# Column norm statistics, a split down projection, a bank-by-bank residual and a reordered router stage in a two-layer MLA and HGRN2 kernel

## The reference, cut to what matters

```python
def rmsnorm(x, g):
    y = x * rsqrt(mean(x * x, -1) + EPS)
    return y * g

for l in range(2):
    mp, ms = ada(c_ctx, w_ada[l], b_ada[l]), ada(c, w_ada[l], b_ada[l])   # silu(c) @ w + b: 6 x 1024 per group
    hp = rmsnorm(xp, norm_mix[l]) * (1 + mp[1]) + mp[0]                   # same for xs with ms
    # l = 0: cq = rmsnorm(h @ w_dq), q = cq @ w_uq, kv = h @ w_dkv, ckv = rmsnorm(kv[:256]), attention, @ w_o
    # l = 1: z, q, i, g from h; chunkwise scan; rmsnorm per head; * silu(g); @ w_o
    xp = xp + mp[2] * yp
    hp = rmsnorm(xp, norm_ffn[l]) * (1 + mp[4]) + mp[3]
    # l = 0: (silu(h @ w1) * (h @ w3)) @ w2;  l = 1: top-2 of 8 experts of softmax(h @ router)
    xp = xp + mp[5] * fp
y_prompt = rmsnorm(xp, final_norm)                                        # same for xs
```

## Time and profile before

| what | value |
|---|---|
| median of three runs | 1766.38 us |
| profiled execution, its own time | 1766.06 us |
| its span | 1764.3 us |
| TensorE, VectorE, ScalarE busy | 94%, 65%, 55% |
| mean granted TensorE clock | 0.971 |
| read from HBM | 489.42 MB |

### The profile page before, as it was taken

One profiled execution on the slowest core, in us unless ns is written; L12 is line 12 of the kernel. 1 busy time (PEld: TensorE's weight loads), 2 busy tenths in 40 slices (PEclk: granted clock), 3 DMA queues, 4 the chain that ended last, 5 costly groups with the idle time before them and its releaser, 6 DMA issues.

```text
span 1764.3 us, 22742 instructions
## 1 busy us (share of the span) xinstructions
PE 1650.6 (94%) x8760; PEld 1323.4 (75%) x8760; DVE 1145.0 (65%) x1098; ACT 963.5 (55%) x976; POOL 36.9 (2%) x35
## 2 busy tenths in 40 slices
PE   5899989999799878889999999999999999999993
PEld 3755779899545667778888888888888888888883
DVE  2126354444311691258898888888888888888886
ACT  1123353333272233257686776777767776777764
POOL 0000000000001010000000000000000000000000
PEclk8999999999899999879999999999999999999997
DMA  9657447775645013069999999999999999999993
GB/s 345 232 176 277 171 151 273 272 260 211 243 143 191 7 44 143 1 209 370 379 375 383 369 375 383 369 379 381 362 391 377 372 383 373 374 384 362 388 367 138
DMA packets 202842, 501.95 MB, mean 285 GB/s; under 512 B 8575, under 2 KB 12062, under 8 KB 188446
## 3 DMA queue, kind: packets, MB, share of 16 engines
q1 hardware_dynamic: 195710, 481.46, 74.3%
q0 software_dynamic: 3664, 13.11, 2.1%
q10 hardware_dynamic: 3408, 6.56, 1.0%
HBM read 489.42 MB, written 11.68 MB: 284 GB/s over the span
## 4 chain that ended last, share of the span: by engine, by line
PE 44%; issue 13%; DVE 6%; ACT 2%; DMA 1%; POOLq 0%; DVEq 0%; ACTq 0%; POOL 0%
PE banks L617 42%; DVE weights_low L1709 2%; DVE ring L1678 2%; PE banks L1046 1%; ACT weights_high L1324 1%; DVE tokens_low L1715 0%; DVE hidden_low L1777 0%; PE banks L1022 0%; DMA pieces<-expert_rows,arena 0%; DVE arena L1773 0%; ACT hT L1120 0%; DMA arena<-token_rows,arena 0%; PE banks L994 0%; DMA arena<-in_state_hgrn 0%; DMA out<-arena 0%
## 5 line engine op out<-in xcount | busy, mean ns | idle before, releaser
L1709 DVE TENSOR_TENSOR weights_low<-pieces,weights_high 128x2048 fp32r<-128x2048 f32 x340 | 763.3, 2288 | 141.4 <-ACT weights_high L1324 141.4
L1324 ACT CAST weights_high<-pieces 128x2048 fp32r<-128x2048 f32 x340 | 632.2, 1912 | 19.9 <-PE banks L617 13.6
L617 PE MATMUL banks<-weights_high,tokens_high 128*128 128x512 f32 x896 | 355.2, 396 | 1.5 <-DVE tokens_low L1715 1.5
L617 PE MATMUL banks<-weights_low,tokens_high 128*128 128x512 f32 x896 | 350.5, 391 | 0.0
L617 PE MATMUL banks<-weights_high,tokens_low 128*128 128x512 f32 x896 | 349.3, 390 | 0.0
L617 PEld LDWEIGHTS banks<-weights_low,tokens_high 128*128 128x128 f32 x896 | 168.6, 188 | 36.2
L617 PEld LDWEIGHTS banks<-weights_high,tokens_high 128*128 128x128 f32 x896 | 169.1, 189 | 34.7 <-issue 1.6
L617 PEld LDWEIGHTS banks<-weights_high,tokens_low 128*128 128x128 f32 x896 | 168.9, 189 | 33.7
L617 PE MATMUL banks<-weights_high,hidden_high 128*128 128x512 f32 x448 | 175.9, 393 | 2.6 <-DVE hidden_low L1777 2.6
L617 PE MATMUL banks<-weights_low,hidden_high 128*128 128x512 f32 x448 | 174.7, 390 | 0.0
L617 PE MATMUL banks<-weights_high,hidden_low 128*128 128x512 f32 x448 | 174.3, 389 | 0.0
(11 more groups left out here) (227 smaller groups left out, 1848.4 us busy)
## 6 DMA issues: line engine op xcount, KB each, us to landing
pieces<-in_moe_w SPq DMA_DIRECT2D x340, 1024.0 KB, 7.5
ring<-in_w_ada SPq DMA_DIRECT2D x24, 2048.0 KB, 9.0
ring<-in_ffn_w SPq DMA_DIRECT2D x15, 2048.0 KB, 8.3
ring<-in_hg_w_f SPq DMA_DIRECT2D x4, 2048.0 KB, 15.2
ring<-in_mla_w_o SPq DMA_DIRECT2D x2, 2048.0 KB, 8.1
ring<-in_hg_w_i SPq DMA_DIRECT2D x2, 2048.0 KB, 14.6
ring<-in_hg_w_q SPq DMA_DIRECT2D x2, 2048.0 KB, 11.1
ring<-in_hg_w_g SPq DMA_DIRECT2D x2, 2048.0 KB, 7.8
```

What stands on the lines that cost most here:

```text
L617: return pe.matmul(o_, lhsT=l, rhs=r, start=start, stop=stop, skip_group_check=True)
L1324: act.copy(parts_hi[:, p % PARTS, :], raw[:, p % RAW, :]).then_inc(rounded, 1)
L1709: dve.tensor_tensor(parts_lo[:, p % PARTS, :], raw[:, p % RAW, :], parts_hi[:, p % PARTS, :].bitcast(F32), ALU.subtract).then_inc(split, 1)
```

## The change

Norm statistics: the squares become the stationary operand and one column of ones the moving one, so the sums of a group stand in one PSUM column with the tokens on the partitions. ScalarE takes the root of 128x2 values straight from PSUM, VectorE the reciprocal, and TensorE spreads it over the partitions again by two products with the identity (`norm_spread`); VectorE reads that from PSUM. ScalarE's table for the root is loaded ahead (`load_root`). Norm 5 stays as it was. Norm 3 writes `x_hi` in the shift itself, and VectorE forms `x_lo` chunk by chunk between the scalings. The start loads `x` first and waits for nothing before the weights; the modulation blocks come in the order 2, 3, 0, then `dq`, then 1, and `dq` is formed in two halves of the features with block 1's step between. The dense residual goes bank by bank, and TensorE no longer waits for all of it. In the router stage the logits come first and are formed chunk by chunk, two pieces rather than four are split ahead, the others after expert 0's tokens, and half of the token rows are turned behind the slot table. The final norm loses a step on VectorE.

```diff
-        add_ada(0, 0, NA_FIRST)
+        ADA_FIRST = (2, 3, 0, 1)
+        add_ada(0, 0, 3)
         add(("dq",), kmaj(a["mla_w_dq"][0], slice(0, QL)))
+        add_ada(0, 3, NA_FIRST)
         add(("dkv",), kmaj(a["mla_w_dkv"][0], slice(0, KVL + ROPE)))
...
+            for g, name in enumerate(("x_prompt", "x_sample")):
+                sp.dma_start(x_rows[:, g, :], a[name][0]).then_inc(rows_in, 16)
             for row, name in ((R_C, "c"), ...
-            for g, name in enumerate(("x_prompt", "x_sample")):
-                sp.dma_start(x_rows[:, g, :], a[name][0]).then_inc(rows_in, 16)
-            sp.wait_ge(consts_in, 16)
-            sp.wait_ge(rows_in, 16 * 11)
...
-                    last = mm(bank[7][:, 0:T], ones[:, :], src[:, k, :], k == 0, k == kc - 1)
+                    for g in range(G):
+                        last = mm(norm_bank[i][:, g:g + 1], src[:, k, P * g:P * g + P], ones[:, 0:1], k == 0 and g == 0, k == kc - 1)
                 last.then_inc(nsum, 1)
+            def norm_spread(i):
+                pe.wait_ge(nrec, NORM_COUNT[i])
+                for g in range(G):
+                    last = mm(norm_bank[i][:, T + P * g:T + P * g + P], inverse[:, g:g + 1].broadcast_to([P, P]), ident, True, True)
+                last.then_inc(nspread, 1)
...
-            for s in range(NA_FIRST + 1):
-                ada_step(0, s, 0, NA_FIRST)
-            (dq: two banks, two halves of a bank, eight chunks each)
+            ada_products(0, 0)
+            norm_spread(0)
+            for s in (1, 2):
+                ada_turn(0, s - 1)
+                ada_products(0, s)
+            ada_turn(0, 2)
+            down_projection(True)      # chunks 0 to 3 of all of dq
+            ada_products(0, 3)
+            ada_turn(0, 3)
+            down_projection(False)     # chunks 4 to 7
...
+                    if f == nf - 1 and c % 2:
+                        last.then_inc(out_done, 1)
-            pe.wait_ge(x_new, 8)
             norm_sums(4, DC, hT)
+            norm_spread(4)
...
             norm_sums(6, DC, hT)
+            norm_spread(6)
+            (logits: for each chunk k, wait h_ready, both groups)
             (h transposes)
-            (logits)
             (rank products)
-            (four groups of token rows)
+            rows(0)
+            rows(1)
             slot_tokens(64).then_inc(rank_ready, 1)
+            rows(2)
+            rows(3)
...
 ScalarE
-            def root(n):
-                act.wait_ge(nrec, n)
-                act.activation(rstd[:, :], rstd[:, :], ACT.Sqrt).then_inc(nroot, 1)
+            def root(i, width):
+                act.wait_ge(nsum, i + 1)
+                act.activation(deviation[:, :], norm_bank[i][:, 0:G], ACT.Sqrt, bias=eps[:, :], scale=1.0 / width).then_inc(nroot, 1)
...
             add_shift(3, 1, 1)
-            act.wait_ge(wo_ready, 8)
-            for p in range(AHEAD):
-                round_piece(0, p)
+            act.activation(unread[:, :], eps[:, :], ACT.Exp)
+            (softmax exponentials)
             (h copies, stores of the token rows)
-            (softmax exponentials)
+            act.wait_ge(wo_ready, 8)
+            for p in range(2):
+                round_piece(0, p)
...
             take_gathered(1, 1)
+            for p in range(2, AHEAD):
+                round_piece(0, p)
...
 VectorE
-                then(dve.tensor_scalar(rstd[:, :], bank[7][:, 0:T], 1.0 / width, EPS, ALU.mult, ALU.add))
-                dve.reciprocal(rstd[:, :], rstd[:, :]).then_inc(nrec, 1)
-                dve.wait_ge(nroot, i + 1 - (i > 5))
+                dve.wait_ge(nroot, NORM_COUNT[i])
+                dve.reciprocal(inverse[:, :], deviation[:, :]).then_inc(nrec, 1)
+                dve.wait_ge(nspread, NORM_COUNT[i])
+                return norm_bank[i][:, T:2 * T]
...
+                    if norm == 1 and c:
+                        dve.wait_ge(x_high, c)
+                        (x_lo of chunk c - 1 = scaled + shift - x_hi, both groups)
...
-            for s in range(NA_FIRST + 1):
-                ada_step(0, s, 0, NA_FIRST)
-            gains(0, 0, NA_FIRST)
-            modulated_norm(0, 0, 0)
+            ada_step(0, 0, 0, NA_FIRST)
+            ada_step(0, 1, 0, NA_FIRST)
+            ada_step(0, 2, 0, 2)
+            gains(0, 0, 2)
+            modulated_norm(0, rstd, 0, 0)
+            ada_step(0, 2, 2, NA_FIRST)
+            ada_step(0, 3, 0, NA_FIRST)
+            ada_step(0, 4, 0, NA_FIRST)
...
-            dve.wait_ge(hid_used, D_FF // P)
-            residual(0, GATE_FFN, 4)
+            residual(0, GATE_FFN, 4, (out_done, 0))
...
-            for p in range(AHEAD):
-                split_piece(0, p)
             dve.wait_ge(lg_ready, 1)
             (softmax, top 2, ranks, slot table)
+            for p in range(2):
+                split_piece(0, p)
             (tokens_low of expert 0)
+            for p in range(2, AHEAD):
+                split_piece(0, p)
```

More of the change, by code:

```diff
@@ L386, in hybrid_step @@
         NA_FIRST = 4
+        ADA_FIRST = (2, 3, 0, 1)
         def add_ada(layer, first, end):
-            for j in range(first, end):
+            for j in (ADA_FIRST[first:end] if layer == 0 and end <= NA_FIRST else range(first, end)):
                 add(("ada", layer, j), kmaj(a["w_ada"][layer], slice(512 * j, 512 * j + 512)))
-        add_ada(0, 0, NA_FIRST)
+        add_ada(0, 0, 3)
         add(("dq",), kmaj(a["mla_w_dq"][0], slice(0, QL)))
+        add_ada(0, 3, NA_FIRST)
         add(("dkv",), kmaj(a["mla_w_dkv"][0], slice(0, KVL + ROPE)))
@@ L687, in _, with down_projection @@
             pe.wait_ge(ada_clear, 1)
-            for s in range(NA_FIRST + 1):
-                ada_step(0, s, 0, NA_FIRST)
[L692 to L696, removed]
-                last.then_inc(cq_ready, 1)
+            ada_products(0, 0)
[4 more added lines that the diff above has]
+            ada_turn(0, 2)
+            def down_projection(first):
+                ks = range(0, DC // 2) if first else range(DC // 2, DC)
+                for j in range(2):
+                    w = have(pe, ("dq",))
+                    for m in range(2):
+                        for k in ks:
+                            pe.wait_ge(h_ready, k + 1)
+                            last = mm(bank[j][:, T * m:T * m + T], w[:, k, P * (2 * j + m):P * (2 * j + m) + P], hT[:, k, :],
+                                      k == 0 and m == 0, k == DC - 1)
+                    if not first:
+                        last.then_inc(cq_ready, 1)
+            down_projection(True)
+            ada_products(0, 3)
+            ada_turn(0, 3)
+            down_projection(False)
             w = have(pe, ("dkv",))
@@ L970, in _ @@
             norm_sums(6, DC, hT)
+            norm_spread(6)
+            pe.wait_ge(router_in, 16)
+            for k in range(DC):
+                pe.wait_ge(h_ready, INPUTS_BEFORE[3] + k + 1)
+                for g in range(G):
+                    last = mm(bank[6][:, NE * g:NE * g + NE], hT[:, k, P * g:P * g + P], router[:, k, :], k == 0 and g == 0, k == DC - 1)
+            last.then_inc(lg_ready, 1)
             for j in range(4):
@@ L988, in _, with rows @@
             mm(bank[7][:, 48:56], ones[:, :], chosen[:, 1, :], False, True).then_inc(rank_ready, 1)
-            for j in range(4):
+            def rows(j):
                 g, q = j // 2, j % 2
@@ L1157, in _ @@
                 if h2 == 3:
-                    root(3)
+                    root(2, KVL)
             for h2 in range(HEADS // 2):
@@ L1324, in round_piece @@
                 act.copy(parts_hi[:, p % PARTS, :], raw[:, p % RAW, :]).then_inc(rounded, 1)
+            load_root()
             x_squares(x_new, 8)
-            root(6)
+            root(6, D)
             add_shift(3, 1, 1)
-            act.wait_ge(wo_ready, 8)
-            for p in range(AHEAD):
-                round_piece(0, p)
+            act.activation(unread[:, :], eps[:, :], ACT.Exp)
+            act.wait_ge(lg_max, 1)
+            for g in range(G):
+                last = act.activation(pr[:, g, :], lg[:, g, :], ACT.Exp, bias=small[:, g, 1:2], accum_out=small[:, g, 2:3])
+            last.then_inc(lg_exp, 1)
             for j in range(4):
@@ L1338, in _ @@
                 act.dma_start(h_rows[P * g:P * g + P, :], h_tok[:, g, :]).then_inc(h_stored, 16)
-            act.wait_ge(lg_max, 1)
-            for g in range(G):
-                last = act.activation(pr[:, g, :], lg[:, g, :], ACT.Exp, bias=small[:, g, 1:2], accum_out=small[:, g, 2:3])
-            last.then_inc(lg_exp, 1)
+            act.wait_ge(wo_ready, 8)
+            for p in range(2):
+                round_piece(0, p)
             for j in range(10):
@@ L1417, in _ @@
                 act.wait_ge(mixed, g + 1)
[L1418 to L1420 removed]
+                then(act.activation(squared[:, g, :], x_tok[:, g, :], ACT.Square, accum_out=small[:, g, 4:5]))
```

(7 more changed lines are left out.)

122 lines of the change are left out of this document (68 added, 54 removed).

## The result

The changed kernel takes 1757.94 us (median of five, 1752.54 to 1758.59), the kernel before, run beside it, 1767.96: a ratio of 0.9941 (0.9927 to 0.9954). It is faster by 10 us, not by the 21 forecast, and 1757.94 lies above the range. The profiled executions are 1757.61 (span 1755.8) and 1766.06 (span 1764.3), 8.5 apart.

The account below looks back on a forecast made before the run. TensorE was taken to bound the expert loop, which the change leaves alone. Terms -2.0 - 1.0 + 0.5 - 1.0 - 9.9 - 7.3 - 0.6 = -21.3 took 1766.06 to 1744.8, forecast 1745 us, range 1736 to 1756.

Parts of the forecast that it names:

- The start: From the first loads to the records behind dkv: -2.0 us forecast, range -5 to +3.5.
- the clock of the sums: One-column norm sums: 3.4 us a norm at the full clock, nothing gained or lost; upper end 6.84 at half.
- Sums end at 18.3: Start: norm 0's sums end at 18.3 us, against 17.23 before, with the rows taken as landing 1 later.
- A modulation step is 1.90 of products: Start: each step takes 1.90 us of products, 0.81 copy and hand-over, 1.16 turning and some 0.2 addition.
- rival (1): One-column sums do not hold the clock; sums and products behind them run at half: +10, 1755 us, chance 15%.
- A third of the 7.8 us is kept: Start: dq begins at 34.2 instead of 42.05, but block 1's step interrupts it, leaving -2.8 us.
- the rows land 0 to 6 us later; I take 1: Start: row loads share the engines with the weights, delaying the rows 0 to 6 us; 1 was taken.
- Norms 1 and 2: Norm 1: shorter chain less slower products, -1.0 us; norm 2: four added records on TensorE, +0.5.
- fed earlier but thinly: Norm 3: scaling starts 1.44 us earlier, but TensorE may run gate and up products at the lower clock: -1.0.
- Norm 4: Residual and sums overlap the last ffn_out, chain 1.36 instead of 2.81 us: -9.9, range -12 to -6.
- the gather took at most 5.5 more: Router: slot table at 758.3, gather done by 763.8; the stage's whole term was -7.3 us, range -9.5 to -3.
- The last norm and the experts: Final norm loses a step and two hand-overs: -0.6 us; experts 0 to 7 stay as long, 959 us.

Follow-up runs that it names:

- wide sums: Changed kernel, but each product of the norm sums streams 128 columns of ones instead of one: 1749.44 us, ratio 0.9894 to the kernel before.
- held loads: Changed kernel, but SyncE issues the load of piece 6 and all behind it only when the first gather has landed: 1753.75 us, ratio 0.9914.
- the residual alone: Kernel before, with only the dense residual taken bank by bank and norm 4's 256-column sums pair by pair in another bank: 1758.19 us, ratio 0.9956.
- all repairs: Changed kernel with 128-column sums, small rows before x, old block order, dq undivided, first splits after gather issue, piece 6 held until gather landed: 1738.19 us.

## Why the prediction was wrong

**The start, 7.4 of the 13 missed.** The step that failed is the clock of the sums: "nothing gained or lost at the full clock, up to 3.4 lost at half. I take the first, as the sums follow dense products". That holds for norms 3 and 6 (3.63 each), but ahead of norm 0 there are only turns of rows and `x`, and its sums took 6.83, the upper end that the prediction had kept. So "Sums end at 18.3" and "A modulation step is 1.90 of products" failed too, and rival (1), which carried the clock, listed only norms 3, 4 and 6 and had 15%. The run with wide sums and the one with held loads begin alike and show what the columns cost here: 5.0 at `dq`'s first product (34.98 against 40.03). Where the first query product is taken it is 6.8 (78.89 against 85.64), as more of the query products run at the lower level.

With wide sums the first record behind `dkv` stands at 68.26: 0.5 behind the kernel before, where the forecast was 2.0 ahead of it. These 2.5 lie along the divided `dq`: it begins 0.8 later than worked out (34.98 against 34.2), its first half takes 9.2 instead of 8.2, and the gap and the rest 24.1 instead of 23.5. "A third of the 7.8 us is kept" also set the division against the wrong kernel. The undivided `dq` was put at 42.05, but without SyncE's wait its blocks come earlier as well, and beside the same wide sums it begins at 38.96. So the division stands against 4, not 7.8, and pays the gap of 5 (right: 50.38 to 55.38) and, in the profiles with the lower clock behind the gap, 1.3 more (19.2 for the 80 products at 49.22 with wide sums, 17.9 in the changed kernel).

That "the rows land 0 to 6 us later; I take 1" was right in size: TensorE begins at 10.13 to 10.55 in the eight profiles with `x` first. It is the order, as the prediction said of its 1, and not the weights: with the small rows first it begins at 9.15 to 9.46 beside the weights and at 8.60 to 9.32 with the waits. The rule of equal turns between queues ("DMA: Bandwidth & Descriptors" of the Trainium skill, section "Queues, rings and completion order") was set aside for a store of 8.2 us; these runs agree with the rule.

**Norms 1 and 2** came in at -1.0 and +0.6, as worked out. The second is no test: the stretch takes 143.7 to 147.4 over the fourteen profiles, 144.9 before, with the clock of the query products in it.

**Norm 3.** The chain is shorter, 5.10 from the first sum to the first scaling against 6.42, but the first gated block is no earlier in any run: 19.45 to 19.75 behind the first sum in all fourteen profiles, whatever the columns. TensorE is "fed earlier but thinly", as the step said, and that took all of the gain, not a part: its records go from 0.41 to 0.28 only at 244.2, 18.3 behind the first sum, before at 236.0, 15.1 behind it.

**Norm 4, 2.6 missed.** Residual and overlap were right; alone they bring 6.9. Missed was the clock: with wide sums the granted clock of this stretch is 0.90, and it is 2.2 shorter (17.63). That leaves 0.4 of the miss.

**The router, 4.0 missed.** The table came 10.3 earlier in the stage, near the 10.9 worked out. The failed step is "the gather took at most 5.5 more": that row was read with VectorE idle and no load in flight, and the change puts two splits and two loads right there. They cost 4.25 and 2.7. With the splits behind the gather the stage is 9.1 shorter than before, more than the 7.3 forecast. The prediction named the queue of loads and asked only whether a piece would be late, not whom the pieces hold up. A rule that spoke against the change was not weighed: "SBUF — State Buffer" of the Trainium skill, section "SBUF: two separate sides", says that VectorE with two inputs in SBUF and a GpSimd operation that reads SBUF lock each other out for a whole instruction. The trace agrees and goes further: the gather did not get in between the two splits either (755.37 to 760.63, splits until 759.74).

**The last norm and the experts** came as forecast. The -2.3 of the scan was not, and it is luck with the clock. From the first `z` to the first sum of norm 6 it takes 246.6 to 246.8 in eight profiles, the residual alone with the scan of the kernel before among them. It takes 248.1 to 249.0 in six, the kernel before among them, and in these six the granted clock falls once between 645 and 660. No edit lies there, and why the clock falls is open.

So of the 8.5 between the two profiles 7.3 are norm 4 and 2.3 are luck, and the other stages together cost 1. With the causes taken away the kernel is at 1738, 27 below the kernel before, where the forecast was 21.

## What to carry over

At the upper clock 32 sums of one column took as long as 32 of 128 (3.77 and 3.74), but here the products behind the narrow ones ran at the lower level: read the price of a narrow product together with that of the dense one behind it. When work is moved, ask what it stands beside in its new place, engine by engine and queue by queue: a duration read from an idle neighbourhood does not move with it. When two edits meet in one stage (here no wait for weights, and a divided `dq`), work out the second against the first, not against the kernel before. Compare two runs stage by stage and look at the clock first: the scan gave 2.3 us to a change that does not touch it.

## What was not expected of the hardware

- 32 products of one column took 6.83 at the lower level without a gap, and the clock was still low behind them; behind 32 of 128 columns in the same place (4.32) it was up.
- The instruction of an indirect DMA on GpSimd took 1.01 with VectorE's splits behind it and 5.26 beside two such subtractions of 4.49 in all.
- With 2 MB weight blocks in flight beside the row loads TensorE began at 9.15 to 9.46, without them at 8.60 to 9.32; but the gathered rows were turned 2.7 later when two 1 MB pieces were loaded beside them.
- Runs of one kernel fall up to 8 us apart (1734.75 to 1742.91 with all repairs, at a mean granted clock of 0.983 to 0.977); an edit of a few us needs several runs and the profile's stage times.
